# The order of the matrix products in the up projection of a two-block transformer kernel

## The reference

```
u = h @ w_up                     # 256 x 1024 @ 1024 x 5632
u = causal 3-tap convolution of u along the tokens + conv_b
a, b = u[..., :2816], u[..., 2816:]
x = x + (silu(a) * b) @ w_down   # 256 x 2816 @ 2816 x 1024
```

## Time and profile before

| | |
|---|---|
| median of 3 runs | 1172.23 us |
| the profiled execution's own time | 1172.82 us |
| its span, first to last instruction | 1170.3 us |
| PE busy | 1158.6 us, 99% |
| PE weight loads busy (beside the products) | 1025.4 us, 88% |
| DVE busy | 932.4 us, 80% |
| ACT busy | 728.5 us, 62% |
| mean granted TensorE clock | 0.998 of full speed |

### The profile page before, as it was taken

One profiled execution on the slowest core, in us unless ns is written; L12 is line 12 of the kernel. 1 busy time (PEld: TensorE's weight loads), 2 busy tenths in 40 slices (PEclk: granted clock), 3 DMA queues, 4 the chain that ended last, 5 costly groups with the idle time before them and its releaser, 6 DMA issues.

```text
span 1170.3 us, 19211 instructions
## 1 busy us (share of the span) xinstructions
PE 1158.6 (99%) x6916; PEld 1025.4 (88%) x6916; DVE 932.4 (80%) x1831; ACT 728.5 (62%) x1349; POOL 6.4 (1%) x13
## 2 busy tenths in 40 slices
PE   9999999999999999999999999999999999999997
PEld 7999989888899888888889988888999898888886
DVE  6998978988888878998887876766799777666666
ACT  5975657666656975776665654545667665455555
POOL 0010000000000000000000000000000000000000
PEclk9999999999999999999999999999999999999999
DMA  8554244554555414655455555454454146455540
GB/s 310 211 195 174 79 174 168 211 211 165 211 179 209 157 55 178 221 203 208 169 206 195 195 206 199 177 197 181 171 192 179 54 165 242 173 204 173 204 162 36
DMA packets 26002, 210.57 MB, mean 180 GB/s; under 512 B 2704, under 2 KB 8080, under 8 KB 9680
## 3 DMA queue, kind: packets, MB, share of 16 engines
q1 hardware_dynamic: 25568, 207.85, 48.9%
q0 software_dynamic: 368, 1.84, 0.5%
HBM read 208.63 MB, written 1.05 MB: 179 GB/s over the span
## 4 chain that ended last, share of the span: by engine, by line
PE 94%; DVE 4%; ACT 2%; issue 0%; POOL 0%; DVEq 0%; ACTq 0%; POOLq 0%
PE ps L450 39%; PE ps L445 18%; PE ps L446 17%; PE ps L447 17%; PE ps L562 1%; DVE w_lo L1795 1%; ACT arena L1204 0%; PE ps L737 0%; DVE arena L2197 0%; ACT w_hi L1204 0%; PE ps L938 0%; DVE arena L2322 0%; DVE h_both L1877 0%; DVE small L2333 0%; PE ps L570 0%
## 5 line engine op out<-in xcount | busy, mean ns | idle before, releaser
L1795 DVE TENSOR_TENSOR w_lo<-raw,w_hi 128x1024 fp32r<-128x1024 f32 (+1 forms) x390 | 446.3, 1162 | 25.5 <-ACT w_hi L1204 25.4
L1204 ACT ACTIVATE w_hi<-raw 128x1024 fp32r<-128x1024 f32 (+1 forms) x390 | 381.8, 1005 | 31.8 <-PE ps L447 27.7
L450 PE MATMUL ps<-h_both,w_hi 128*128 128x512 f32 x1088 | 386.8, 398 | 0.0
L450 PE MATMUL ps<-h_both,w_lo 128*128 128x256 f32 x1088 | 305.4, 281 | 0.0
L450 PEld LDWEIGHTS ps<-h_both,w_hi 128*128 128x128 f32 x1088 | 204.4, 188 | 50.0
L450 PEld LDWEIGHTS ps<-h_both,w_lo 128*128 128x128 f32 x1088 | 205.4, 189 | 2.6
L445 PE MATMUL ps<-w_hi,y_hi 128*128 128x512 f32 (+1 forms) x518 | 204.6, 395 | 1.0 <-DVE y_lo L2247 0.8
L446 PE MATMUL ps<-w_lo,y_hi 128*128 128x512 f32 (+1 forms) x518 | 201.7, 389 | 0.0
L447 PE MATMUL ps<-w_hi,y_lo 128*128 128x512 f32 (+1 forms) x518 | 201.0, 388 | 0.0
L1204 ACT ACTIVATE arena<-ps 128x256 f32<-128x256 f32 (+2 forms) x166 | 57.7, 396 | 148.6 <-PE ps L450 139.9
L445 PE MATMUL ps<-h_both,w_hi 128*128 128x256 f32 x520 | 148.3, 285 | 0.0
(11 more groups left out here) (292 smaller groups left out, 1314.6 us busy)
## 6 DMA issues: line engine op xcount, KB each, us to landing
raw<-in_stream SPq DMA_DIRECT2D x125, 1536.0 KB, 6.5
raw<-in_stream SPq DMA_DIRECT2D x2, 1152.0 KB, 10.7
raw<-in_stream SPq DMA_DIRECT2D x3, 512.0 KB, 7.0
raw<-in_stream SPq DMA_DIRECT2D x4, 384.0 KB, 6.9
x<-in_x SPq DMA_DIRECT2D x2, 512.0 KB, 5.0
arena<-in_mem SPq DMA_DIRECT2D x1, 1024.0 KB, 13.3
raw<-in_stream SPq DMA_DIRECT2D x1, 1024.0 KB, 7.2
x<-in_x POOLq DMA_DIRECT2D x1, 1024.0 KB, 5.1
```

The costliest lines, as they stand in the source:

```text
L450: return pe.matmul(o, l, r, start=start, stop=stop, skip_group_check=True)
L1204: return act.activation(o, i, ACT.Copy, scale=scale)
L1795: dve.tensor_tensor(w_lo[:, s, a], raw[:, s, a], w_hi[:, s, a], ALU.subtract).then_inc(s_lo, 1)
```

## The change

In `up_both` the products of a half are issued in another order. The first half issues its eight 512-column products in a row and then its eight 256-column ones; the second half issues its eight 256-column products first and then its eight 512-column ones. The flag that clears the bank (`start`) goes to the first product of a half and the flag that ends the sum (`stop`) to its last. The number of products, their operands, their banks, the waits ahead of each half and the semaphore at the end of the chunk stay.

```diff
                 def up_both(j, z):
                     s, b = (U0 + j) % SLOTS, half_bank(j, z)
+
+                    def high(k, start, stop):
+                        a = slice(z * PIECE + k * P, z * PIECE + k * P + P)
+                        return full(ps[:, b, :], w_hi[:, s, a], h_both[:, k, :, :].rearrange("p a b -> p (a b)"), start, stop)
+
+                    def low(k, start, stop):
+                        a = slice(z * PIECE + k * P, z * PIECE + k * P + P)
+                        return full(ps[:, b, 0:S], w_lo[:, s, a], h_hi[:, k, :], start, stop)
+
+                    first, last = (low, high) if z else (high, low)
                     for k in range(KT):
-                        a = slice(z * PIECE + k * P, z * PIECE + k * P + P)
-                        full(ps[:, b, :], w_hi[:, s, a], h_both[:, k, :, :].rearrange("p a b -> p (a b)"), k == 0, k == KT - 1)
-                        m = full(ps[:, b, 0:S], w_lo[:, s, a], h_hi[:, k, :], False, k == KT - 1)
+                        first(k, k == 0, False)
+                    for k in range(KT):
+                        m = last(k, False, k == KT - 1)
                     return m
```

## The result

The changed kernel takes 1165.2 us (median of 6 runs, 1164.95 to 1165.97) against 1172.43 for the kernel before (6 runs, 1171.9 to 1174.88): a ratio of 0.9938, 95% interval 0.9927 to 0.9948. Faster was forecast, by 6.8 us to 1165.4. The profiled execution took 1165.15 us with a span of 1163.4; the span before was 1170.3, so 6.9 us less.

The account below looks back on a forecast made before the run. PE was taken as the bound, by the distances between its products' starts. 0.10 us less per chunk times 68 chunks gives 6.8 us, from the median 1172.23 to 1165.4 us; range 1163.8 to 1167.8 (8 in 10).

Parts of the forecast that it names:

- PE's distances between starts are the path: FFN chunks: PE busy 1158.6 of 1170.3 us, so every nanosecond between two products' starts sets the end.
- The prices of steady steps, carried from the chunks that aren't alternated: Chunk 20 of FFN 0 and its down: 0.1200 us per 256-column product, 0.2267 per 512, against 0.3533 an alternated pair.
- The price of the one change down and up that is left: Per chunk: a change down in width gives back 0.01 us, one up costs 0.03, together 0.02.
- The sum: A chunk with its down: 8.385 to 8.288 us, 0.097 less, taken as 0.10; times 68 chunks, 6.8 us.
- The excess as a property of products: Rival: high products of `up_both` take 0.2367 us themselves, a pair 0.3533 in any order; 1172.2 us; chance 6%.
- DVE's round: Rival: DVE sets the pace in FFN 0 and 1, its round at most 8.07 us; gain 3.8 us, 1168.4; chance 3%.
- Weight loads in the open: Rival: in sixteen short products, loads of 0.189 us set the step; 68 us more, 1240; chance 3%.
- A distance by a product's own columns alone: Opposing skill rule: N / 2.4 + 2.5 ns, 109 ns for 256 columns, 216 for 512; order worth nothing, 1172.2 us.
- an alternation is sixteen changes each way, each with a price: Chunk's up: sixteen width changes down and sixteen up cost 0.12 us excess; one of each leaves 0.02.

Follow-up runs that it names:

- all-256 run: Kernel before, still alternating, with the 512-column product of `up_both` cut to 256 columns (`w_hi h_lo` alone), so both products are short: 1085.14 us, one run.
- all-512: Kernel before, still alternating, with the 256-column product of `up_both` widened to 512 columns (it adds `w_lo h_lo`): 1281.51 us, one run.
- run without the mirror: Changed kernel, but both halves issue their eight 512-column products first and their eight 256-column ones after: 1167.05 us, ratio 0.995.
- 128-column runs: Low products of 128 columns instead of 256, in the old alternated order and in the changed order: 1159.34 us and 1159.82 us, one run each.
- rows of two: Changed kernel, but each half issues two 512-column products, two 256-column ones, and so on: 1166.35 us, ratio 0.9942.
- rows of four: Changed kernel, but each half issues four 512-column products, then four 256-column ones, twice: 1169.84 us, one run.

## Why the prediction was right

*PE's distances between starts are the path.* Right: PE's waits between engines didn't change, DVE and ACT had room (the all-256 run puts the pace that DVE allows at 7.8 to 8.0 us a chunk, under the prediction's 8.07), and the 0.100 us per chunk came out whole in the span, 6.8 of 6.9 us.

*The prices of steady steps, carried from the chunks that aren't alternated.* Right to the nanosecond: 226.7 and 120 in the new rows of eight and sixteen, but for the first steps behind a change. The all-512 and all-256 runs show that it was sound to carry them from other tensors and other banks.

*The price of the one change down and up that is left, 0.02 us.* Right, 20 ns, and it moved, as said, from down's first products into the second half's high ones. The run without the mirror confirms it with a second pair of changes: 20 ns more. Its exactness is in part luck: it was made of 0.01 given back and 0.03 paid, read from starts with two decimals, where the starts in ns give 7 and 27; the two roundings cancel.

*The sum.* 0.10 us was taken and 0.100 measured, though the first of its two ways gave 0.097: it started from 8.385 us a chunk, where the starts in ns give 8.387; 6.8 us forecast and 6.9 measured in the span, 7.2 between the medians of 6 runs. The range from 1163.8 to 1167.8 held.

*The excess as a property of products.* False, by the first high products after down and by the all-512 run. *DVE's round.* False: no wait of PE came up. *Weight loads in the open.* False at 256 columns: sixteen low steps of 120 ns with loads from `w_lo` alone. The 128-column runs show how near something like it lies: a floor of some 0.112 us, 8 ns under the low step of this kernel, whose cause is open. In the terms of that rival, the load's record of 0.189 us was never the price.

*A distance by a product's own columns alone* would have given 1172.2; the measured 1165.2 goes against it. The Trainium skill states such a rule ("TensorE: Matmul & The Clock Gate", section "Back-to-back issue gap") for a product taken by itself, with some 109 ns for 256 columns. For a stream of loads and products the same section gives 131 ns for 512 columns, which the prediction left out. This case agrees with neither: 256 columns take 120 ns in a row and 112 to 120 by their neighbours, 512 columns 227 in a row.

*What the prediction had and the runs took away* is the reading that an alternation is sixteen changes each way, each with a price. The number of changes and the excess don't go together (rows of two: 26 ns with eight; rows of four: 86 ns with four). The forecast didn't rest on it, since both ends of its comparison were measured, the alternated pair as a whole and the settled change as a whole; any interpolation between them would have been wrong, and was, in the expectations for rows of two and of four.

Open is why an order costs what it costs. Shown is that a mix of widths is needed, and that the tensor of the weights, the bank and the neighbours' operands don't matter. The steps repeat within 1 ns from chunk to chunk with a period of three pairs in alternation, and a chunk takes the same time in FFN 0 and 1 as in FFN 2 and 3, where DVE has less to do; so it is a fixed property of the sequence, not contention with another engine. No run shows the mechanism.

## What to carry to other kernels

Where PE bounds a kernel, read the distances between the starts of its products and look for a stretch where the same shape stands in a row of equals: the difference times the count is what an order is worth. Here that gave the fall of the span to 0.1 us. Prices of two measured orders can't be interpolated to a third: each order has to be measured as a whole, and one chunk of it is enough, since the steps repeat. Letting a row run on into the neighbouring stage with the same width was worth 20 ns a chunk here. Longer rows aren't better in themselves, since rows of two beat rows of four. At 128 columns, near the floor, the order was worth nothing.

## What was not expected of the hardware

- Rows of two are better than rows of four, and than rows of eight without the mirror: excess of 120, 26, 86 and 40 ns a chunk for rows of one, two, four and eight. With the mirror rows of eight have 20.
- A change up from 256 to 512 columns costs 27 ns over five steps after a long row, but a visit of two 512s and two 256s on the way cuts the pair of changes from 20 ns to 6; the version with it has the shortest span of those with the full computation, 1162.7 us, though its runs overlap those of the changed kernel.
- A low product of 448 columns beside one of 512 costs more excess a pair, 10 ns by the estimated step of 0.200 us, than one of 256, 7 ns.
- Products of 1, 64 and 128 columns, each with its own weight load, all follow each other after some 112 ns in a row, almost the 120 of 256 columns. Halving the low products' width took 8 ns off a step, and leaving half of the low work out was worth 94 ns a chunk, 6.4 us over 68 chunks; the runs fell by 5.4 us in the rows (1165.2 to 1159.8, one run), with a wait of PE of 1.9 us that the changed kernel doesn't have.
